# Decay-sum and beta rows held at four partition groups, for the spreading products of a gated-delta pair

## What is computed

```
proj = a @ w_in                                  # a: (T, 1024), w_in: (1024, 7184)
beta = sigmoid(proj[..., OFF_BETA:OFF_A])        # (T, 8): one per head
g    = -exp(a_log) * softplus(proj[..., OFF_A:OFF_GLU] + dt_bias)   # (T, 8)
gc   = cumsum(g) within chunks                   # decay sums, per head
decay = exp(where(tril, gc[..., :, None] - gc[..., None, :], -inf))
kb   = k * beta[..., None]
qg   = q * exp(gc)[..., None]
# then, per head and chunk: t_inv = inverse(I + strict(kb k^T * decay)), u, w, outputs, state
```

## Time and profile before

| | us |
|---|---|
| median of 3 runs | 1479.61 |
| lowest and highest | 1477.51 and 1480.71 |
| the profiled execution's own time | 1477.59 |
| its span in the profile | 1475.9 |

### The profile page before, as it was taken

How to read it: one execution, slowest core, us unless ns; L and a number is a source line. 1 busy time by engine, 2 the same in 40 slices (tenths; PEclk the granted TensorE clock), 3 DMA queues, 4 the chain that set the end, 5 groups by cost and what they waited for, 6 DMA issues and landing times.

```text
span 1475.9 us, 20370 instructions
## 1 busy us (share of the span) xinstructions
PE 1362.0 (92%) x7693; PEld 781.6 (53%) x7693; DVE 461.1 (31%) x1012; ACT 297.4 (20%) x636; POOL 22.7 (2%) x53
## 2 busy tenths in 40 slices
PE   8999897999999999899898898988989989999887
PEld 6787776778887434434344243342443434434256
DVE  2566776764224402202022021120220202202214
ACT  4544544444213001000010010000100101101024
POOL 2000000000000000000000000000000000000000
PEclk8999999999999999999999999999999999999999
DMA  7324333333493999999999999999999999999950
GB/s 210 104 87 132 103 102 103 103 103 102 167 368 130 396 422 421 422 422 422 422 421 420 421 421 422 422 421 423 422 420 420 421 422 422 421 421 421 421 190 30
DMA packets 121523, 462.77 MB, mean 314 GB/s; under 512 B 10843, under 2 KB 69748, under 8 KB 72196
## 3 DMA queue, kind: packets, MB, share of 16 engines
q1 hardware_dynamic: 105147, 451.97, 76.6%
q10 hardware_dynamic: 16305, 9.82, 2.3%
HBM read 455.75 MB, written 6.68 MB: 313 GB/s over the span
## 4 chain that ended last, share of the span: by engine, by line
PE 68%; DMA 21%; DVE 5%; ACT 3%; issue 2%; SPq 0%; ACTq 0%; DVEq 0%
DMA ring<-in_w_gate_up 21%; PE bank L1154 15%; PE bank L1112 14%; PE bank L939 10%; PE bank L1070 6%; PE bank L1175 4%; PE bank L986 3%; PE bank L1020 2%; PE bank L1226 2%; PE bank L762 2%; PE bank L1105 1%; PE bank L1134 1%; PE bank L768 1%; DVE lent L1875 1%; PE bank L1090 1%
## 5 line engine op out<-in xcount | busy, mean ns | idle before, releaser
L1112 PE MATMUL bank<-ring,lent 128*64 128x512 f32 (+1 forms) x2304 | 459.3, 595 | 66.3 <-DMA ring<-in_w_gate_up 66.1
L1112 PEld LDWEIGHTS bank<-ring,lent 128*64 128x64 f32 (+1 forms) x2304 | 148.0, 131 | 362.0 <-issue 343.0
L939 PE MATMUL bank<-lent,ring 128*128 128x264 f32 x896 | 228.0, 395 | 3.8 <-DVE big L1895 1.6
L1154 PE MATMUL bank<-ring,lent 128*64 128x512 f32 (+1 forms) x1152 | 226.7, 595 | 0.2 <-ACT lent L1599 0.2
L939 PEld LDWEIGHTS bank<-lent,ring 128*128 128x128 f32 x896 | 162.5, 192 | 37.5 <-issue 9.5
L2047 DVE TENSOR_SCALAR big<-bank 128x512 f32<-128x512 f32 x32 | 20.6, 686 | 431.4 <-PE bank L1112 431.4
L1154 PEld LDWEIGHTS bank<-ring,lent 128*64 128x64 f32 (+1 forms) x1152 | 69.8, 131 | 135.9 <-issue 128.7
L1593 ACT ACTIVATE big<-big 128x512 f32<-128x512 f32 x32 | 19.6, 630 | 511.9 <-DVE big L2047 511.9
L1070 PEld LDWEIGHTS bank<-st,big 88*128 88x128 f32 x768 | 87.0, 192 | 12.8 <-issue 11.4
L1070 PE MATMUL bank<-st,big 88*128 88x128 f32 x768 | 90.0, 277 | 0.6 <-ACT outputs L1590 0.5
L2065 DVE TENSOR_TENSOR xT<-xT,bank 128x264 f32<-128x264 f32 x128 | 54.9, 429 | 96.8 <-PE bank L1175 95.3
(11 more groups left out here) (392 smaller groups left out, 1071.2 us busy)
## 6 DMA issues: line engine op xcount, KB each, us to landing
ring<-in_w_gate_up SPq DMA_DIRECT2D x256, 1024.0 KB, 19.0
ring<-in_w_down SPq DMA_DIRECT2D x128, 1024.0 KB, 23.4
ring<-in_w_in SPq DMA_DIRECT2D x28, 1024.0 KB, 5.3
out<-st ACTq DMA_DIRECT2D x8, 512.0 KB, 5.2
ring<-in_w_gdn_out SPq DMA_DIRECT2D x4, 1024.0 KB, 5.1
ring<-in_w_out SPq DMA_DIRECT2D x4, 1024.0 KB, 10.0
ring<-in_w_ple_gate SPq DMA_DIRECT2D x4, 1024.0 KB, 15.6
st<-in_state_gdn ACTq DMA_DIRECT2D x6, 512.0 KB, 4.1
```

Source lines behind the costliest of these rows:

```text
L939: last = mm(b[:, 0:T], w[:, k, o:o + P], aT[:, k, :], start=k == 0, stop=k == KD - 1)
L1112: last = mm(bank[t][lo:hi, :], x_slots[:, c, lo:hi], w, start=False, stop=c == KD - 1)
L1154: last = mm(bank[4 + t][lo:hi, :], hT[:, m, lo:hi], w, start=m == 0, stop=m == KD - 1)
```

## The change

Both sets of rows are now held more than once. A tile `rows4` of 128 partitions replaces `rows8` of 8: betas at partitions 0 to 7 and again at 64 to 71, decay sums at 32 to 39 and again at 96 to 103. `sel8` is held at the same four groups. The four spreading products of a pair take their operands from partitions 32, 0, 96 and 64, in this order. The sigmoid and both copies are done twice, the copy of `sel8` four times.

```diff
-        sel8 = sbuf("sel8", [H, H, P])
+        sel8 = sbuf("sel8", [P, H, P])
...
-        rows8 = sbuf("rows8", [H, 2, T])
-        betaT, gcF = rows8[:, 0, :], rows8[:, 1, :]
+        rows4 = sbuf("rows4", [P, T])
+        gcF = [rows4[q:q + H, :] for q in (32, 96)]
+        betaT = [rows4[q:q + H, :] for q in (0, 64)]
...
-                        for x, src in (("bcg", gcF), ("bcb", betaT)):
+                        for x, src, row in (("bcg", gcF[j], 64 * j + 32), ("bcb", betaT[j], 64 * j)):
                             b = to_fill(pe, name(f"{x}{j}"))
-                            fill_done(name(f"{x}{j}"), mm(b[:, 0:T], sel8[:, 2 * g + j, :], src, start=True, stop=True))
+                            fill_done(name(f"{x}{j}"), mm(b[:, 0:T], sel8[row:row + H, 2 * g + j, :], src, start=True, stop=True))
...
-                    tell(A(betaT, b[0:H, 0:T], ACT.Sigmoid))
+                    for x in betaT:
+                        tell(A(x, b[0:H, 0:T], ACT.Sigmoid))
...
-                    tell(v.tensor_copy(gcF[:, TP:T], gT[:, TP:T]), "gcF_ready")
+                    tell(v.tensor_copy(gcF[0][:, TP:T], gT[:, TP:T]))
+                    tell(v.tensor_copy(gcF[1][:, TP:T], gT[:, TP:T]), "gcF_ready")
...
-                    out_of(v.tensor_copy(gcF[:, 0:TP], b[0:H, 0:TP]), "gcf")
+                    tell(v.tensor_copy(gcF[0][:, 0:TP], b[0:H, 0:TP]))
+                    out_of(v.tensor_copy(gcF[1][:, 0:TP], b[0:H, 0:TP]), "gcf")
...
-            tell(g_.tensor_copy(sel8[:], ident[0:H, 0:H].unsqueeze(2).broadcast_to([H, H, P])), "consts")
+            for q in range(4):
+                r = slice(32 * q, 32 * q + H)
+                tell(g_.tensor_copy(sel8[r, :, :], ident[r, r].unsqueeze(2).broadcast_to([H, H, P])), "consts" if q == 3 else None)
```

More of the change, by code:

```diff
@@ L743, in early_step @@
                     b = to_fill(pe, "gbt")
-                    for i, src in enumerate((gT, gT, betaT, betaT)):
+                    for i, src in enumerate((gT, gT, betaT[0], betaT[0])):
                         last = tr(b[:, i * H:(i + 1) * H], chunk(src, i % 2), ident[0:H, 0:H])
```

## The result

| | before | after |
|---|---|---|
| median of 12 runs | 1478.88 us | 1480.68 us |
| their range | 1476.78 to 1480.86 | 1478.98 to 1483.52 |
| profiled execution | 1477.59 | 1479.05 |
| its span | 1475.9 | 1477.3 |
| mean granted clock of an execution | 0.992 (110 executions, those beside the experiments) | 0.988 (12 executions) |

The change makes the kernel 0.16% slower: the ratio is 1.0016 (95% interval 1.0009 to 1.0024). The time lies in the predicted range and within the 0.2% that the prediction called no change. But the interval leaves out "no change", which was the forecast, and so a cause is to be found.

The account below looks back on a forecast made before the run. In the experts, weight arrival bounds (DMA share 1.01), their start moving with PE. PE's 4.50 us saving was lost waiting for ACT and setup was hidden: change 0, forecast 1479.6 us, range 1477.0 to 1482.4.

Parts of the forecast that it names:

- The products overlap: Spreading products: four row groups overlap fully, saving 0.54 us in pair 0 and 1.32 in each other pair, 4.50 in all.
- the four separate signals: Each spreading product signals its own bank; three more in a row take about 0.08 us off each group's saving.
- The gain is hidden behind ACT: PE's projection-bank waits behind the spreading products grow to 0.74, 2.50, 2.93, 1.95 us; gain on the path 0, chance 0.80.
- The doubled setup is hidden: ACT's second sigmoid, DVE's second copies and POOL's three copies add nothing; without covers the ACT and DVE work is 1.06 us.
- The direct covers: ACT idle 2.93 us before L1341, DVE idle 1.29 us at 54.63, and PE's signal at 44.35 not later.
- Hidden, both.: DVE's idle 1.29 us at 54.63 covers its 256-column copy, about 0.45 us; ACT's second sigmoid, 0.41, was also called hidden.
- The clock: Rival: clock falls behind the longer waits of pairs 1 to 3, up to 1.70 us each; 1484.7 us, 0.34% slower, chance 0.08.
- PE's wait of 1.78 us at 172.22: PE's wait for DVE soon after pair 1's wait, claimed to make up most of a clock fall there.
- The range: From 1477.0 us, two of four savings passed on, to 1482.4, one clock fall (1.70) and early terms uncovered (1.06).
- 1.06 us of setup work uncovered at the start: ACT's second sigmoid 0.41 us and DVE's second copies 0.20 and 0.45, if nothing covered them.

Follow-up runs that it names:

- the filled kernels: Change with all four lengthened waits filled by products of ones, against the doubled setup alone, both on the filled base: medians 1476.51 and 1476.21 us.
- the filled base: All kernels given products of ones in TensorE's other long waits (17, 8, 17, 10); before, with 3, 5, 2 in projection waits too: 1475.48 us, ratio 0.9985.
- the kernel with pairs 1 and 3 filled: The change on the filled base with 9 and 7 products of ones in the waits of pairs 1 and 3 only: 1476.57 us, ratio 0.9991.

## Where the prediction was right and where it failed

**The products overlap, right.** The group took 0.72 us in pair 1 where 0.65 was worked out, and 1.49 in pair 0 where 1.43 was. The saving is 0.48 in pair 0 and 1.26 in each of the others (2.44 - 1.18, 2.87 - 1.61, 1.89 - 0.63), 4.3 us in all, not 4.50. The missing 0.06 to 0.07 in each group is near what the four separate signals were to cost by the page of the Trainium skill, TensorE: Matmul & The Clock Gate, section "The cost: per-tile semaphore tail" (an estimate of 0.08). No run separates these signals from other costs of a group, so the agreement is weak.

**The gain is hidden behind ACT, right.** The waits were to be 0.74, 2.50, 2.93 and 1.95 and are 0.69, 2.44, 2.87 and 1.89. That the packed products are worth nothing is also shown by the filled kernels (-0.07 us, -0.85 to 0.66).

**The doubled setup is hidden, half right.** The direct covers held: PE's wait for the gains is 2.37 us with it and 2.38 without. The failing step is the sentence "Hidden, both.": it weighed the time of the added instructions and not their number. Three more instructions shift what comes after in the lists of ACT and DVE, and waits of 0.25 and 0.17 us appear 240 and 350 us later.

**The clock, wrong where it was weighed.** The mechanism stood there, with its places and the price of one fall: up to 1.70 us, and 1.66 and 1.49 were measured. What failed is "I hold one or two falls to be as likely as not, and their cost to be mostly absorbed." and, ahead of it, that PE's wait of 1.78 us at 172.22 would make up for a fall in pair 1. I had read the length of the next wait and not what its releaser waits for. DVE's L1800 hangs on PE's own products, and so the wait moves with PE. Of the falls behind lengthened waits only pair 2's is absorbed. Nor had I looked at pair 3, whose next wait is 0.35 us. With the 2.3 us that the four waits cost together and 0.4 for the two small ones, where the prediction had 0, the sum would have been 1479.6 + 2.3 + 0.4 = 1482.3. The difference of the medians is 1.8 us, and the ratio says 2.4 (1.3 to 3.5). On the filled base the same comparison gives 1478.49 - 1475.16 = 3.3.

**The range** held, and partly by luck: its upper end took in one unabsorbed fall and 1.06 us of setup work uncovered at the start, and what came was about one and a half falls' price and 0.4 us of setup in another place. The chance of 0.08 for the clock was too low for what rows 7 and 8 showed: after a wait of 2.38 us the clock had fallen, and two waits were to become longer than that.

**Left open.** It is open in how many executions the clock falls behind pair 1's wait, since only profiled ones show it: behind 2.44 or 2.45 us it fell in one of three, behind pair 3's shorter wait of 1.89 in four of four. In the kernel before the wait of 1.78 us at 172.22 left the clock at 1.00; in five kernels of the filled base, before with its waits filled among them, the same wait near 167 was followed by a fall, and in three others not. In the kernel with pairs 1 and 3 filled the waits of 0.94 and 0.17 us behind it took this fall up but for some 0.2 us. So the length of a wait alone does not decide. And 0.3 to 0.7 us of the doubled setup on the filled base were measured and not placed.

## What to carry to other kernels

Time saved on an engine that then waits is not free of effect: if a wait of TensorE grows (here to between 1.89 and 2.87 us), look for a clock fall behind it, and count its price wherever the next waits end by something that hangs on TensorE itself. A wait absorbs a delay only if its releaser does not depend on what is late, so follow the releaser one step back. Where a wait can't be removed, products of ones into an unused bank kept the clock up behind it: in the kernel before, without the change, seven waits filled so brought 0.15% (0.06 to 0.24). Three of the seven alone brought nothing that can be told (0.9994, 0.9984 to 1.0004).

## What the runs showed of the hardware

- A clock fall came behind TensorE's waits of 1.89 us (in four of four profiled executions), 2.45 us (in one of three) and 2.87 us (in five of five), for 3.4 us or twice that. One of 3.4 us cost 1.49 and 1.66 us where nothing took it up.
- The run-to-run spread of the kernel before, 6 us, goes with its mean granted clock (from 1475.44 us at 0.994 to 1480.76 at 0.990). With TensorE kept busy in seven waits the standard deviation is 0.92 us (11 runs) in place of 1.63 (33 runs).
- Adding three one-column instructions near the start of ACT's and DVE's programs gave TensorE waits of 0.25 and 0.17 us hundreds of microseconds later; with fifteen the one of ACT sat elsewhere and that of DVE was not seen. Differences of 0.4 us between two kernels may be no more than that.
